# A transformer block's attention computed from transposed scores, with row maxima from rounded operands, and one convolution chunk's tap products made on ScalarE

## The reference

```python
s_loc = jnp.einsum('bnqkgd,bnjkd->bnkgqj', qb, kw).astype(jnp.float32) * scale
s_ctx = jnp.einsum('bnqkgd,bckd->bnkgqc', qb, kc).astype(jnp.float32) * scale
s_loc = jnp.where(valid[None, :, None, None], s_loc, -jnp.inf)     # |qpos - kpos| <= 128
p = jax.nn.softmax(jnp.concatenate([s_loc, s_ctx, sl], axis=-1), axis=-1)   # sl: one sink per head
o = (jnp.einsum('bnkgqj,bnjkd->bnqkgd', p_loc, vw)
     + jnp.einsum('bnkgqc,bckd->bnqkgd', p_ctx, vc))
...
s = jnp.einsum('bqkgd,bjkd->bkgqj', q, k).astype(jnp.float32) * (HEAD_DIM ** -0.5)   # global: all keys
p = jax.nn.softmax(s, axis=-1)
...
u = dwconv(a * jax.nn.sigmoid(g), w) + bias           # 31 taps, 256 channels
return jax.nn.silu(layer_norm(u, ln_g, ln_b))
```

## Time and profile before

| | us |
|---|---|
| median of 3 runs | 3902.67 |
| lowest and highest | 3902.58, 3907.64 |
| the profiled execution's own time | 3902.73 |
| its span | 3900.9 |
| `attend` of layer 0, on TensorE | 326.5 to 590.0 |
| `attend` of layer 1, on TensorE | 1638.2 to 1859.6 |

### The profile page before, as it was taken

The page is one execution under the profiler, slowest core; times in us unless marked ns, Lnnn a source line. Parts: engine busy times, 40 slices in busy tenths (PEclk is TensorE's granted clock), DMA queues, the critical chain, the costliest instruction groups (busy, mean ns, idle before and its releaser), DMA issues. The chain is left out here.

```text
span 3900.9 us, 41076 instructions
## 1 busy us (share of the span) xinstructions
PE 3302.3 (85%) x16972; PEld 1921.7 (49%) x16972; DVE 1055.7 (27%) x2000; ACT 659.3 (17%) x1275; POOL 440.3 (11%) x636
## 2 busy tenths in 40 slices
PE   3799998479999938999758777479998998879997
PEld 0456773323333303577332111168785586748875
DVE  0225542321111122443130000132324266222232
ACT  0111120100000111111100000032222155122231
POOL 1006700011111110170001111100000000000000
PEclk7896558589999968855869999889999979989998
DMA  9131000369999891100249999912312100132130
GB/s 393 39 97 44 1 0 11 140 234 389 385 388 391 308 374 54 65 1 1 78 172 413 414 412 412 371 54 87 108 58 97 65 1 1 65 113 87 65 119 27
DMA packets 141428, 637.02 MB, mean 163 GB/s; under 512 B 11824, under 2 KB 19008, under 8 KB 86000
## 3 DMA queue, kind: packets, MB, share of 16 engines
q1 hardware_dynamic: 121104, 575.58, 37.4%
q0 software_dynamic: 20192, 59.58, 5.0%
HBM read 611.95 MB, written 23.17 MB: 163 GB/s over the span
## 5 line engine op out<-in xcount | busy, mean ns | idle before, releaser
L897 PE MATMUL bank<-slots,HT 128*32 128x512 f32 x4096 | 479.1, 600 | 79.3 <-DMA slots<-in_w_up_dram 41.5
L667 PE MATMUL bank<-slots,HT 128*128 128x512 f32 (+2 forms) x960 | 400.7, 578 | 20.4 <-ACT done_mark L1531 20.4
L897 PEld LDWEIGHTS bank<-slots,HT 128*32 128x32 f32 x4096 | 121.7, 110 | 400.8 <-issue 243.4
L667 PEld LDWEIGHTS bank<-slots,HT 128*128 128x128 f32 x960 | 182.4, 192 | 230.3 <-issue 204.5
L667 PE MATMUL bank<-hT_high,chunk_high 128*128 128x512 f32 x704 | 277.3, 394 | 8.3 <-DVE low_slots L1922 8.3
L667 PE MATMUL bank<-hT_high,low_slots 128*128 128x512 f32 x704 | 277.7, 395 | 0.0
L667 PE MATMUL bank<-hT_low,chunk_high 128*128 128x512 f32 x704 | 276.9, 393 | 0.0
L916 PE MATMUL bank<-arena,HT 128*32 128x512 f32 x2048 | 243.9, 596 | 26.7 <-DMA arena<-in_w_down_dram 26.2
L698 PE MATMUL bank<-ident,arena 128*128 128x128 f32 x272 | 61.0, 402 | 223.0 <-DVE arena L1593 145.5
L667 PE MATMUL bank<-HT,slots 128*128 128x512 f32 (+1 forms) x480 | 172.3, 521 | 1.7 <-ACT done_mark L1531 1.7
L698 PEld LDWEIGHTS bank<-ident,arena 128*128 128x128 f32 x272 | 50.2, 212 | 237.5 <-issue 198.8
(11 more groups left out here) (323 smaller groups left out, 4431.0 us busy)
## 6 DMA issues: line engine op xcount, KB each, us to landing
slots<-in_w_gate_dram SPq DMA_DIRECT2D x128, 1024.0 KB, 8.6
slots<-in_w_up_dram SPq DMA_DIRECT2D x128, 1024.0 KB, 11.0
arena<-in_w_down_dram SPq DMA_DIRECT2D x128, 1024.0 KB, 13.2
slots<-in_ada_w_dram SPq DMA_DIRECT2D x24, 2048.0 KB, 22.2
slots<-in_w_in_dram SPq DMA_DIRECT2D x15, 2048.0 KB, 13.0
slots<-in_ffn_w_gate_dram SPq DMA_DIRECT2D x10, 2048.0 KB, 8.5
slots<-in_ffn_w_up_dram SPq DMA_DIRECT2D x10, 2048.0 KB, 8.8
slots<-in_ffn_w_down_dram SPq DMA_DIRECT2D x10, 2048.0 KB, 7.8
```

Of the source, the lines that this page charges most:

```text
L667: mm = pe.matmul(out_, lhsT, rhs, start=(n == 0), stop=(n == len(pairs) - 1))
L897: mm = pe.matmul(bank[32 * j:32 * j + 32, 2 + n, :], xT[:, kk0 + kk, lo:lo + 32], w[n][:, kk, 512 * h:512 * h + 512], start=(pair == 0 and ...
```

## The change

The attention of the first block is laid out anew (`attention_plan`). Instead of units it has groups: one kind, one key/value head with its two query heads, and all main queries (512) or all context queries (256). Layer 0 has four context groups, then four main groups; layer 1 four main groups; global (kind 1) groups come ahead of window groups. A group has two parts.

- Row maxima. For each query tile and head (8 `units` for a main group, 2 for a context group) TensorE computes the scores with queries on the partitions as before, for main groups from copies of Q and K rounded to fp32r (`q_round`, `k_round`), which ScalarE makes. VectorE reduces them to maxima, negates them, TensorE turns these into one row (`turn_shift`, 1x128 transposes), and ScalarE puts the row into partition 64 of the extended queries (`Q_ext`), whose counterpart in the extended keys (`K_ext`) is 1.
- Steps, one for each key tile (6 for a main group, 2 for a context group). TensorE computes the scores transposed, keys on the partitions, 65 rows contracted, up to 512 columns; ScalarE takes the exponential straight into `probT`; TensorE multiplies the extended V (`V_ext`, 64 columns of V beside 64 of ones) with it, up to 512 columns, so that the sums come out in the other half of the partitions. A sink is added by one more matmul.

No probabilities are turned any more, and no row sums are made by ScalarE. At the end of a group ScalarE copies sums and values out (`take_outcome`), and VectorE takes the reciprocal of the 128x512 sums and multiplies. The row maxima of a group are worked on two groups ahead in layer 0 and one ahead in layer 1, spread over the steps, through one pair of banks (4 and 5).

Of the long convolution, ScalarE now makes the products of chunk 0 (`make_taps`, a ring of four), GpSimd only adds them, and does the short convolution afterwards instead of first. In `qkv`, ScalarE writes Q and K by eight copies for each tile instead of two, and GpSimd sets the constant rows. SP issues the loads of `w_out` only once attention has ended, since `Q_ext` lies in their slots.

```diff
+def attention_plan(layer):
...
+    ahead = 2 if layer == 0 else 1
...
+                if number < ahead:
+                    unit.pair = (4, 0, 2, 6)[units % 4]
...
             for stage in stages:
+                if stage.name == "attend":
+                    attended = stage.at("mixed", stage.signals["mixed"])
+                if stage.name == "w_out":
+                    sp.wait_ge(sem["mixed"], attended)
...
+                def row_scores(unit):
...
+                    b = unit.pair
+                    if unit.previous is not None:
+                        pe.wait_ge(sem["rowmax_free"], st.at("rowmax_free", unit.previous + 1))
...
+                    kT = k_round[st.layer][0:HD + 1, group.kind, group.g, :]
+                    q = q_round[st.layer][0:HD + 1, group.kind, group.heads + unit.j, tile_cols(qt)]
...
+                        pe.matmul(bank[:, b, :], q, kT[:, 0:SEQ], start=True, stop=True)
...
+                    pe.matmul(bank[:, b + 1, 0:CTX], q, kT[:, SEQ:NTOK], start=True, stop=True).then_inc(sem["rowmax_full"], 1)
...
+                def turn_shift(group):
+
+                    pe.wait_ge(sem["neg_max"], st.at("neg_max", group.number + 1))
...
+                            mm = pe.transpose(bank[0:1, 4 + j, tile_cols(i)], small[:, c:c + 1], ident[:, :])
+                    mm.then_inc(sem["shift_full"], 1)
...
+                    if one.first:
+                        pe.wait_ge(sem["shift_done"], st.at("shift_done", group.number + 1))
...
+                        mm = pe.matmul(bank[:, b, 0:one.hi - one.lo], keys, q_ext[0:HD + 1, group.kind, group.heads + j, one.lo:one.hi],
+                                       start=True, stop=not edges)
...
+                        mm = pe.matmul(bank[:, 6 + j, lo:hi], V_ext[:, one.kt, group.kind, at_v:at_v + P], p,
+                                       start=one.first, stop=ends)
...
+                    for n, one in enumerate(group.steps):
+                        if n + 1 < len(group.steps):
+                            scores(group.steps[n + 1])
+                            for unit in units[share * n:share * n + 1]:
+                                row_scores(unit)
+                        else:
+                            if later:
+                                turn_shift(later)
+                            if group.number + 1 < len(groups):
+                                scores(groups[group.number + 1].steps[0])
+                        mix(one)
...
+                    for j in range(2):
+                        y, sums = slice(HD * j, HD * j + HD), slice(HD * (1 - j), HD * (1 - j) + HD)
+                        act.wait_ge(sem["mixed"], st.at("mixed", 2 * group.number + 1 + j))
+                        act.activation(total[y, 0:n], bank[sums, 6 + j, 0:n], ACT.Copy).then_inc(sem["mixed_taken"], 1)
...
+                            if made >= 4:
+                                act.wait_ge(sem["tap_added"], st.at("tap_added", made - 3))
...
+                            act.activation(products[:, made % 4, 0:hi - lo], conv_b_in[:, 0, at_k:at_k + hi - lo], ACT.Copy,
+                                           scale=conv_b_w[:, st.layer, 0, k:k + 1]).then_inc(sem["tap_made"], 1)
...
+                        for _ in one.parts:
+                            next(ready_taps, None)
...
+                    dve.wait_ge(sem["mixed_taken"], st.at("mixed_taken", 4 * group.number + 4))
+                    step(dve.reciprocal(total[:, 0:n], total[:, 0:n]))
+                    y = HT[:, 4 + 2 * group.kind + group.g, cols]
+                    dve.tensor_tensor(y, y, total[:, 0:n], ALU.mult).then_inc(sem["total_read"], 1)
...
+                        pool.wait_ge(sem["tap_made"], st.at("tap_made", n + 1))
+                        if k:
+                            pool.wait_ge(sem["tap_added"], st.at("tap_added", n))
+                        other = dst if k else conv_vec[:, 0, l, 0:1].broadcast_to([P, hi - lo])
+                        pool.tensor_tensor(dst, other, products[:, n % 4, 0:hi - lo], ALU.add).then_inc(sem["tap_added"], 1)
```

514 lines of the change are left out of this document (331 added, 183 removed).

## The result

| | before | after |
|---|---|---|
| time, median of 4 runs each, us | 3905.15 | 3778.6 |
| lowest to highest, us | 3902.58 to 3908.72 | 3776.27 to 3785.96 |
| profiled span, us | 3900.9 | 3774.5 |
| start of the mean behind attention (L667 before, L753 after), layer 0 | 590.0 | 541.5 |
| the same, layer 1 | 1859.6 | 1731.7 |

The changed kernel is faster: its time is 0.9679 of the time before, with a 95% interval of 0.9661 to 0.9696. The forecast was 3759 with a range of 3695 to 3865. The time lies in the range and 20 us above the forecast. Of the 126.4 us that the span lost, layer 0's attention gave 48.5 (forecast 53.8), the way from there to the end of layer 1's attention 79.4 (forecast 89.5 for layer 1), and 1.4 came back behind it.

What follows compares the result with a forecast made beforehand. TensorE, at 1.2 GHz with its clock granted at 0.50, was taken to bound both attention stages. Layer 1 -90.0, qkv copies +0.5 and layer 0 -53.8 make -143.3, so 3902.7 becomes 3759 us; range 3695 to 3865.

Steps and rivals of the forecast that it cites:

- The clock in the main groups: TensorE's clock in both layers' main groups: high, near 1.00, because 512-column matmuls are denser; float32 records 0.43 us apart.
- Rival 3: Slower: clock never rises in attention, 65-row scores counting as 64-row ones did; +54 us, 3957; chance 0.11.
- Layer 1: Layer 1's attention: opening 17.4, groups 25.8, 31.6, 30.8 and 25.7; 131.3 us against 221.3, -90.0.
- row-copy waits: Layer 1, between groups: TensorE's next scores wait for ScalarE's copy of the row, 1.3, 2.3 and 2.3 us.
- hand-over waits: Between groups: TensorE's second row unit waits for VectorE's maximum, which stands behind copies, reciprocal and product; 2.9 us each.
- rival 2: Attention: clock falls at hand-overs and returns late, main groups losing 9 or 10 us each; +90, 3850; chance 0.15.
- Layer 0: Layer 0's attention: 182.5 us of opening and groups plus GpSimd's end, 208 against 263.5; -53.8 with qkv's copies.
- GpSimd's tail: End of layer 0's attention: GpSimd adds three taps, then does the short convolution; conv_out waits 25.5 us.
- Edits at nothing: Later w_out loads covered by conv_out, GpSimd's constant rows hidden in qkv, later stages' clock starts unchanged: no cost.
- The lock: VectorE's taps between maxima: skill's port lock would add 40 us; the sum used the trace's median, 0.39 above 0.74.
- TensorE-bound: Attention: VectorE and ScalarE keep ahead of TensorE; layer 1 is 120 us, layer 0 163, total 3704; chance 0.09.
- The rival of no change: Whole kernel: gains and GpSimd's tail cancel, clock between rivals' levels, nothing measurable changes; chance 0.03.

Runs made afterwards that it cites:

- e9: Changed kernel with short convolution in GpSimd's gaps, VectorE's outcome one group later, and all scores over 128 rows (63 zero) instead of 65: 3727.4 us.
- e1: Changed kernel with GpSimd's short-convolution chunks in its two layer 0 gaps between tap sums instead of last: 3763.9 us.
- e5: Changed kernel with GpSimd making its own tap products again and the short convolution first, ScalarE making none: 3788.3 us.
- e7: Changed kernel with a group's last products put ahead of the next group's first scores on TensorE in layer 1: 3781.1 us.
- b1: Kernel before, keys of each head written over 128 rows with zeros in the other head's 64, so scores contract over 128: 3693.8 us.
- c1: Kernel before with scores contracting over all 128 rows of data instead of 64 (computes another thing): 3702.5 us, one run.

## Why the prediction was nearly right, point by point

- **The clock in the main groups.** Right in effect (1.00 in long stretches, 512-column float32 records 0.43 apart), wrong in its reason. The prediction held that the new work is denser and the old one sparse, with 2.6 of 6.8 us in weight loads. The old work at 128 rows is as sparse and runs at 0.94; the new work with twice the instructions keeps 0.87. What the earlier trace rows showed, and the prediction passed over, is a TensorE that was busy all the time at 0.50 with `64*128` in its rows. The earlier trace rows pointed there too: of its windows, the one at 0.50 with 4.00 of 4 us busy held 64-row scores, and the one at 1.00 96-row scores. The prediction read the growth of columns out of them. The rows are not the whole of it either: in the same stage 64-row scores ran at 1.00 from 3160.6 on, until TensorE had waited 2.1 us at 3169, and the clock came back from 3212 with 64-row scores still in the mix. Rival 3 named the 64 rows; it expected 65 rows to fare as badly, which they do only in part: the clock is high in long stretches, and e9 shows that it rises sooner and is low for less time with 128 rows in all of them. That the products of 128 rows beside them keep it high is likely; no run takes them away. The forecast of a high clock was thus right, by luck as far as its reason goes.
- **Layer 1: 141.0 us from the stage's start, forecast 131.3.** The opening to the first scores took 14.4 (1590.7 to 1605.1), as forecast. The row-copy waits were 1.1, 2.2 and 2.2 (forecast 1.3, 2.3, 2.3), the hand-over waits 2.4 and 1.5 (forecast 2.9 each). The step that failed is the clock behind these waits: the sum gave it 3 us at the start and nothing at the hand-overs. The first group was 4.8 us longer than forecast (33.6), the second 3.7 (35.3), the third 2.6 (33.4), the last 1.4 shorter (24.3). So the mechanism of rival 2 was there, at 3 to 5 us a group and not at the 9 to 12 that it priced.
- **Layer 0: down 48.5, forecast 53.8.** Opening 14.2 (13), the first two context groups 24.7 (22), the third 24.4 (23.9), the fourth and the main groups 126.9 (123.6). The size of the context groups is right by luck, since the mechanism is another: VectorE alone was to set 2.2 us a unit; in the trace a unit takes 2.06 because TensorE (1.03 at the low clock) and VectorE (0.96) take turns on one pair of banks, with the tap under TensorE's part. Taps were cheaper than the 1.13 taken (0.78 in the third and fourth context group, 1.05 behind), since GpSimd now pauses for ScalarE.
- **GpSimd's tail.** Forecast 25.5, measured 24.7, and e1 shows it to be a real price of the change: 14.7 us of it could be had back.
- **Edits at nothing.** They held. `w_out` of layer 0 starts 21.0 us behind the mean (541.5 to 562.5), before 21.9; nothing waited for its load.
- **The lock.** The prediction weighed a rule of the Trainium skill, "SBUF — State Buffer", "SBUF: two separate sides", that VectorE and GpSimd lock the port that they share for an instruction and the loser blocks, and went by a shorter tap. In the changed kernel that was right, because GpSimd pauses. In e5, where it doesn't, the 6.01 us product fits the rule and goes beyond it: it lasted through nine instructions of GpSimd, not one. That the lock is what held it is argued and not shown.
- **Rivals.** TensorE-bound (3704) had no wait at the hand-overs and no fall there, and kept GpSimd's tail; e9, with that tail and the hand-overs' waits for VectorE gone and the falls shorter, is still at 3727. The rival of no change and the slower one did not come.

## What to carry to other kernels

Look at the rows that the matmuls use before rebuilding a stage that is at half clock with TensorE busy: here two more key copies with zeros gave 211 us of 3905, and the whole rebuild of the attention 127. After a rebuild, ask what each engine has left at the end (GpSimd's short convolution) and what stands ahead of the first thing that TensorE needs at a boundary (a 3.35 us reciprocal): these two orders were worth 32 us. With both and with 128 rows the new layout is at 3727, and the old one, with 128 rows and ScalarE's products, at 3679. And a wait that is covered hands over to the next wait in the row, as e7 shows, unless that one is looked up first.

## What was not expected of the hardware

- TensorE's clock stayed at 0.50 with the engine busy 99 per cent of 264 us, on scores that use 64 of 128 rows beside full-height transposes and products; the same program with 128 rows in the scores ran at 0.89 to 1.00 between the ends of its stages, with zeros in the added rows (b1) as with data (c1). The Trainium skill, "TensorE: Matmul & The Clock Gate", "Part 1: The HAM clock gate", describes a monitor that sets the clock by how busy the array has been. The trace agrees only in part: a busy engine was not enough here.
- A VectorE product of 0.69 us lasted 6.01 beside a GpSimd that ran without a pause (one instance, and no other product of that size met a busy GpSimd in layer 0's main groups); maxima that read PSUM were not slowed (0.95 us in both).
- Traces of the same layer-0 program ended its attention 6.2 us apart; runs of one kernel differed by 20 us (e1, 3752.2 to 3771.9) and by 32 (e5, 3785.4 to 3817.8), while the kernel before, run beside them, stayed within 11 (3900.0 to 3910.7). That it is the moment at which the clock rises and falls is likely, and not shown.
